# A two-block transformer on one core: the second layer's norm and projection stream by stream, its low-rank chunk third, its convolution later, two ring slots lent, and output products tile by tile

## What is computed

```python
# layer 0 (even): both streams            # layer 1 (odd)
z = h @ w_in                              # h: RMS norm of x, times (1+scale), plus shift
o = window_attention(q, k, v)             # layer 1: mla_q / mla_kv: low-rank parts are RMS-normed, then @ w_uq / @ w_ukv, rope
s = spatial_gating(...)                   # layer 1: gb * conv3(gc * hh)   (gated_short_conv)
x = x + gate * (concat([o, s]) @ w_out)
h = rms_norm(x) * (1 + m4) + m3
x = x + m5 * expert_choice_ffn(h)         # 16 experts, each takes its 32 best tokens of a stream
```

## Time and profile before

| | us |
|---|---|
| median of 3 runs | 2333.02 (2328.42 to 2338.51) |
| the profiled execution | 2334.52 |
| its span | 2332.7 |
| PE busy | 1998.7 (86%) |
| VectorE busy | 1002.4 (43%) |
| ScalarE busy | 749.3 (32%) |
| DMA | 643.78 MB, mean 276 GB/s |

### The profile page before, as it was taken

How to read it: one execution, slowest core, us unless ns; L and a number is a source line. 1 busy time by engine, 2 the same in 40 slices (tenths; PEclk the granted TensorE clock), 3 DMA queues, 4 the chain that set the end, 5 groups by cost and what they waited for, 6 DMA issues and landing times.

```text
span 2332.7 us, 37883 instructions
## 1 busy us (share of the span) xinstructions
PE 1998.7 (86%) x16424; PEld 1492.7 (64%) x16424; DVE 1002.4 (43%) x1908; ACT 749.3 (32%) x1338; POOL 11.3 (0%) x24
## 2 busy tenths in 40 slices
PE   5999899989897889766565656999999999998998
PEld 4777655444443757644444434878888877887887
DVE  3346522222221645411110104665576757556776
ACT  3344310000000625200000003655454546654544
POOL 0000000000000000000000000000000000000000
PEclk9999999999999999888788887999999999999999
DMA  9867379999999523599999995334545443345551
GB/s 398 319 233 308 147 304 427 427 427 427 427 427 427 230 95 124 229 426 427 426 426 427 426 426 230 145 145 148 204 176 194 181 155 134 145 181 190 185 200 66
DMA packets 46147, 643.78 MB, mean 276 GB/s; under 512 B 5232, under 2 KB 5504, under 8 KB 6560
## 3 DMA queue, kind: packets, MB, share of 16 engines
q1 hardware_dynamic: 43776, 628.75, 66.7%
q0 software_dynamic: 2208, 12.62, 1.4%
HBM read 640.30 MB, written 1.05 MB: 275 GB/s over the span
## 4 chain that ended last, share of the span: by engine, by line
PE 64%; DMA 29%; DVE 3%; ACT 2%; issue 1%; SPq 0%; ACTq 0%; DVEq 0%; POOLq 0%
PE bank L918 60%; DMA ring<-in_stream 29%; PE bank L926 3%; DMA arena<-in_b_masks 0%; DVE weights_low L2490 0%; DVE tokens_low L2053 0%; ACT arena L1880 0%; DVE arena L2590 0%; ACT ring L1755 0%; DVE ring L2293 0%; ACT weights_high L1592 0%; ACT arena L1624 0%; DVE x L2104 0%; DVE arena L2220 0%; ACT arena L1613 0%
## 5 line engine op out<-in xcount | busy, mean ns | idle before, releaser
L918 PE MATMUL bank<-ring,arena 128*32 128x128 f32 (+4 forms) x7704 | 621.7, 379 | 213.3 <-DMA ring<-in_stream 208.4
L918 PEld LDWEIGHTS bank<-ring,arena 128*32 128x32 f32 (+1 forms) x7704 | 366.3, 134 | 439.1 <-DMA ring<-in_stream 265.0
L2490 DVE TENSOR_TENSOR weights_low<-ring,weights_high 128x1024 fp32r<-128x1024 f32 (+2 forms) x288 | 343.5, 1195 | 271.9 <-ACT weights_high L1592 268.4
L1592 ACT ACTIVATE weights_high<-ring 128x1024 fp32r<-128x1024 f32 (+2 forms) x288 | 297.7, 1035 | 283.3 <-PE bank L918 282.7
L918 PE MATMUL bank<-weights_high,tokens_high_low 128*128 128x512 f32 (+2 forms) x1152 | 359.2, 386 | 10.7 <-DVE tokens_high_low L2502 8.8
L918 PEld LDWEIGHTS bank<-weights_high,tokens_high_low 128*128 128x128 f32 x1152 | 215.1, 189 | 55.9 <-DVE tokens_high_low L2502 9.2
L1592 ACT ACTIVATE arena<-bank 128x256 f32<-128x256 f32 (+6 forms) x254 | 104.5, 435 | 389.7 <-PE bank L926 301.7
L918 PE MATMUL bank<-weights_low,tokens_high_low 128*128 128x512 f32 (+2 forms) x576 | 218.9, 380 | 0.0
L2210 DVE TENSOR_TENSOR arena<-arena,bank 128x256 f32<-128x256 f32 (+1 forms) x64 | 22.7, 355 | 446.2 <-PE bank L918 446.2
L1716 ACT ACTIVATE arena<-bank 128x256 f32<-128x256 f32 (+1 forms) x64 | 21.2, 331 | 572.9 <-PE bank L918 572.9
L2220 DVE TENSOR_TENSOR arena<-bank,arena 32x512 f32<-32x512 f32 (+1 forms) x128 | 70.8, 553 | 254.0 <-PE bank L918 252.7
(11 more groups left out here) (216 smaller groups left out, 2107.4 us busy)
## 6 DMA issues: line engine op xcount, KB each, us to landing
ring<-in_stream SPq DMA_DIRECT2D x298, 2048.0 KB, 21.8
arena<-in_stream POOLq DMA_DIRECT2D x7, 1024.0 KB, 9.7
x<-in_x_in SPq DMA_DIRECT2D x1, 2048.0 KB, 10.6
arena<-in_od_pack POOLq DMA_DIRECT2D x1, 1024.0 KB, 13.1
x<-in_stream POOLq DMA_DIRECT2D x1, 1024.0 KB, 13.7
arena<-in_gains POOLq DMA_DIRECT2D x2, 512.0 KB, 5.9
out<-arena SPq DMA_DIRECT2D x1, 1024.0 KB, 4.0
arena<-in_b_masks POOLq DMA_DIRECT2D x1, 896.0 KB, 9.6
```

What stands on the lines that cost most here:

```text
L918: ins = pe.matmul(o, lhsT, rhs, start=start, stop=stop)
L1592: ins = act.activation(o, i, ACT.Copy)
L2490: dve.tensor_tensor(dst, whole, high.bitcast(F32), ALU.subtract).then_inc(sig, 1)
```

## The change

The bank table, the order of odz and the ring:

```diff
-ADDS_AT = 42
+ADDS_AT = 40
-ODZ_ORDER = (1, 2, 3, 4, 0)
+ODZ_ORDER = (1, 2, 0, 3, 4)
+ODZ_BANKS = {1: (0, 1), 2: (6, 7), 0: (0, 1, 2, 3), 3: (4, 5), 4: (6, 7)}
+CTX_TURNS = (1, 3)
+LORA_SQUARES, LORA_ROOTS, LORA_SCALES, LORA_ROPE = (2, 3, 4), 5, (6, 7), 1
-RING_SLOTS = (3, 1, 4, 5, 0, 2)
-B2_SLOTS = (0, 2, 3, 1)
+RING_SLOTS = {"moe0": (3, 1, 4, 5, 0, 2), "odd": (2, 3, 1, 0), "moe1": (2, 3, 4, 5, 1, 0)}
+B2_SLOTS = (1, 0, 2, 3)
-OD_WEIGHTS = ((13312, 14336), (7040, 19456), (6528, 22016))
+OD_WEIGHTS = ((7040, 19456), (6528, 22016))     # the third buffer lies in the ring
+od_zb, od_q, od_xn = spare(...)                 # in slots 4 and 5
```

Output products, the last three pieces of c=1 tile by tile (mix0 and mix1), and VectorE's order behind mix0:

```diff
+            def z_tail(name, c):
+                ks = range(KD - LAST_TOGETHER, KD)      # LAST_TOGETHER = 3
+                for t in range(tiles):
+                    for k in ks:
+                        if t == 0:
+                            pe.wait_ge(sem("z_w_lo"), Z_AT[name, c, k] + 1)
+                        ...three products of tile t...
+                used(name, c)
             for t in range(4):
                 mix_add("mix0", 1, t)
-            scaled(X, moe_xn, 4, 8)
+                if t:
+                    scaled(X, moe_xn, 4, 8, [t - 1])
+            scaled(X, moe_xn, 4, 8, [3])
```

From the experts to the projection. PE: the gate rows come in front of the last combine; 16 transposes of the main stream, and those of the context behind piece (1, 3):

```diff
                     elif what == "comb":
+                        if layer == 0 and g == GROUPS - 1:
+                            for n in range(4):
+                                v = 2 + 3 * (n // 2)
+                                mod_row("modrow1", n, mrow[:, 2 * v * P:(2 * v + 2) * P], 0)
                         combine(g)
-            norm("n1_1", xn4, 4, sem("xn"), 12)
+            stream_turns("n1x", 0)
             for what, c, k in odz_schedule():
                 if what == "w":
                     z_product("odz", c, k)
-                    if (c, k) == (0, 2):
-                        convolution()
+                    if (c, k) == CTX_TURNS:
+                        stream_turns("n1c", TT)
```

ScalarE (VectorE has the like: four adds, scale tile 0, two adds, scale tile 1, two adds; `stream_split("n1x")`; scale tiles 2 and 3):

```diff
-            square_sums(X, moe_xn, 4, lambda t: x_done(act, 0, t))
+            b.drained("moe0", (GROUPS - 1, PER_GROUP - 1, "y"))
             for n in range(4):
                 mod_row("modrow1", n)
-            b.drained("modcol1", 1)
-            norm_split("n1_1", A1[1], B1[1], 8, Z_FIRST["odz"])
+            square_sums(X, od_xn, 4, lambda t: x_done(act, 0, t), range(TT))
+            stream_split("n1x", 0, 8)
+            square_sums(X, od_xn, 4, lambda t: x_done(act, 0, t), range(TT, 4))
             for what, c, t in odz_schedule():
                 if what == "w":
                     if not early_split("odz", c, t):
                         z_split("odz", c, t)
+                    if (c, t) == (CTX_TURNS[0], CTX_TURNS[1] + 2):
+                        stream_split("n1c", 1, 16)
+                    if c == 3 and t in LORA_SQUARES:
+                        ...two of the six square sums...
+                    if (c, t) == (3, LORA_ROOTS):
+                        ...two roots...
+            def stream_split(name, s, tok):
+                cols = slice(s * SEQ, (s + 1) * SEQ)          # 256 columns: one stream
+                for half in range(2):
+                    j = 2 * half                              # VectorE: bank j + 1
+                    b.filled(name, j)
+                    for k in (2 * j, 2 * j + 1):
+                        if half:
+                            act.wait_ge(sem("z_tok_lo"), tok + k - 3)
+                        ...scale and shift of k...
+                    for k in range(4 * half, 4 * half + 4):
+                        b.drained(name, k // 2)
+                        copy(z_hi[:, k, cols], z_tokens[:, k % 4, cols], sem("z_tok_hi"))
+                        if s == 0 and k == 1:
+                            ...the two early weight pieces...
```

VectorE scales the low-rank parts at (3, 6) and (3, 7) and ropes the key at (4, 1). Behind the projection PE turns the low-rank parts, then does the convolution, then `uq`:

```diff
+            convolution()
             uq = chunk("odz", 4)[...]
+            pe.wait_ge(sem("conv_done"), TT)                 # in front of attention
+            owed.extend(SPARE_SLOTS)                         # slots 4 and 5 go back
```

More of the change, by code:

```diff
@@ L263, in _tickets @@
             stage("modcol0", [0], LAST_BANK)
[L264 to L267, removed]
+            norm("n1_0")
             for p in range(A_END):
@@ L359, in put @@
         SLOT_OF.append(slot)
-    ring = itertools.cycle(RING_SLOTS)
+    ring = {name: itertools.cycle(slots) for name, slots in RING_SLOTS.items()}
     for c in range(MOD_EARLY):
@@ L378, in _chunks @@
     for key in in_ring + [("mix1", c) for c in range(2)] + [("moe1", k) for k in range(6 * N_EXP)]:
-        put(key, None if key in EXTRA else next(ring))
+        put(key, None if key in EXTRA else next(ring.get(key[0], ring["odd"])))
     first = len(SLOT_OF)
@@ L403, in freed_for @@
 def freed_for(n):
[L405 removed]
+    lent = (SLOT_OF[n] in SPARE_SLOTS) * ((n >= CHUNK_AT["moe0", 0]) + (n >= CHUNK_AT["moe1", 0]))
+    return LOADS_OF[n] - 1 + lent
 def b2_chunk(name, k, layer):
@@ L432, in z_before, with in_tail @@
     return n - Z_BUFS[name] if n - Z_BUFS[name] >= Z_FIRST[name] else None
+LAST_TOGETHER = 3
+def in_tail(name, c, k):
+    return name in ("mix0", "mix1") and c == 1 and k >= KD - LAST_TOGETHER
 def z_width(name, c):
@@ L2018, in _, with scaled @@
             dve.memset(mrow, 0.0).then_inc(sem("mod_clear"), 1)
-            def scaled(x, xn, tiles, n_root):
-                for t in range(tiles):
+            def scaled(x, xn, tiles, n_root, which=None):
+                for t in range(tiles) if which is None else which:
                     dve.wait_ge(sem("root"), n_root - tiles + t + 1)
@@ L2222, in gated_out, with combined @@
                     ins.then_inc(frees(moe, (g, e, "y")), 1)
-                def combined(g):
-                    for n in range(2 * tiles):
+                def combined(g, which=range(2 * tiles)):
+                    for n in which:
                         t, c = n // 2, n % 2
@@ L2237, in experts @@
                         gathered(g)
+                    elif what == "comb" and (layer, g) == (0, GROUPS - 1):
+                        combined(g, range(4))
+                        scaled(X, od_xn, 4, 12, [0])
+                        combined(g, range(4, 6))
+                        scaled(X, od_xn, 4, 12, [1])
+                        combined(g, range(6, 8))
                     elif what == "comb":
@@ L2421, in _ @@
[L2421 to L2426 removed]
+                    if (c, k) == (CTX_TURNS[0], CTX_TURNS[1] + 2):
+                        stream_split("n1c", 1, 16)
@@ new lines, in _ @@
+                    if c == 3 and k in LORA_SCALES:
+                        if k == LORA_SCALES[0]:
+                            dve.wait_ge(sem("lora_root"), 2)
+                            steps.do(dve.reciprocal(rstd2[:, :], ss2[:, :]))
+                        for n in range(3):
+                            lora_scale(3 * LORA_SCALES.index(k) + n)
+                    if (c, k) == (4, LORA_ROPE):
+                        dve.wait_ge(sem("od_in2"), 16)
+                        x = od_za[:, :, KV_LORA:KV_LORA + KR]
+                        tmp = [spare(SPARE_RTMP + 32 * m, TT, 16) for m in range(4)]
+                        rope(x[:, :, 0:16], x[:, :, 16:32], od_cos, od_sin, tmp, sem("od_krope"))
+                        dve.wait_ge(sem("od_krope"), 1)
@@ L2441, in _ @@
                 dve.tensor_copy(kf[:, :, 64:96], over_heads(src, OD_HEADS, KR)).then_inc(sem("od_kr"), 1)
+            for t in range(TT):
+                for part in range(3):
+                    convolve(t, part)
             b.drained("uq", (1, 1))
```

154 lines of the change are left out of this document (99 added, 55 removed).

## The result

| | kernel before | changed kernel | ratio, 95% interval |
|---|---|---|---|
| median of the first measurement (4 runs each) | 2331.07 us | 2315.69 us | 0.9924 (0.9905 to 0.9944) |
| median of the second (9 and 5 runs) | 2333.41 us | 2317.29 us | 0.9927 (0.9915 to 0.9940) |
| span of the profiled execution | 2332.7 us | 2313.8 us | |

What follows compares the result with a forecast made beforehand. Expert stages were taken as bound by the weight stream, so reaching them earlier moves everything after. Gains 3.8 + 2.7 + 5.8 + 0.7 = 13.0 us gave 2320.0 us; the forecast's own range 2315 to 2325, over the cases 2311 to 2330.

Steps and rivals of the forecast that it cites:

- Steps 1: End of mix0: last three pieces run tile by tile, first router norm eviction 3.8 us earlier, bounds 2.5 to 4.5.
- step 5: Low-rank part and convolution, projections' end to first uq eviction: 9.35 us instead of 15.2, gain 5.8, bounds 3.5 to 6.5.
- step 7: Ring of weight slots: two slots lent, cost 0, both expert stages as long as now; 5 to 10 us if chunks were missing.
- Step 6: End of mix1: same tile-by-tile tail with two tiles, gain 0.7 us, bounds 0 to 1.2.
- Step 2: Last expert product to first projection: gate rows before combine, norm split by streams; third piece at 776.8 instead of 781.5, 4.7 gained.
- Step 3: Context stream inside c=1: 1.9 us transposes, 2.7 wait, 1.9 half clock; c=1 ends at 793.4 instead of 791.6.
- Step 4: Projection chunks 2, 0, 3, 4: c=3 1.1 us late from low-rank squares; projections end at 839.0 instead of 841.7, 2.7 gained.
- dearer handoffs: Rival for the projection: ScalarE/VectorE waits come to 11 us instead of 3 + 2.7, 8 lost, 2328; chance 0.15.
- The router's gain: Rival: the router's 3.8 us do not pass on, expert stream bound by loads issued before, 2324; chance 0.06.
- stay at 1.2 GHz: Slower rival: PE stays at 1.2 GHz from piece 2 on, each piece waiting for its weights, 2344; chance 0.08.
- wait elsewhere: Last rival: the squares wait elsewhere and only the low-rank part moves, 2327; chance 0.03.
- hole in the clock: Rival inside c=1: transposes act as a hole in the clock, 12 products by 0.2 us, 2322.5; chance 0.06.

Runs made afterwards that it cites:

- experiment 1: Changed kernel with only the last piece of mix0 and mix1 made for all tiles together again; median 2319.85 us, ratio 0.9950.
- experiment 8: Changed kernel with unused products in PE's two gaps, three before the first projection product and four before the third piece; median 2316.81 us, ratio 0.9930.
- experiment 9: Changed kernel with the low-rank squares, roots, scalings and key's rope behind the whole projection again, convolution left in place; median 2324.48 us, ratio 0.9959.
- experiment 4: Changed kernel with the gate rows behind the combine again and their ScalarE copies behind the squares; median 2317.83 us, ratio 0.9941.
- experiment 5: Changed kernel with the context stream's transposes and split up front, behind the main stream's, instead of inside c=1; median 2313.50 us, ratio 0.9913.
- experiment 7: Changed kernel with the context stream's squares, transposes and halved split spread under the first two projection chunks; median 2310.48 us, ratio 0.9902.
- experiment 2: Kernel before with only the tile-by-tile ends of mix0 and mix1 and scalings between the adds; median 2331.00 us, ratio 0.9989.
- experiments 3: As experiment 2, plus three unused products in PE's wait before the combine; median 2329.71 us, ratio 0.9986.
- 10: As experiment 7, plus three unused products ahead of the first projection product; median 2308.73 us, ratio 0.9891.

## Why the prediction was right, and where it was not

The mechanism held. The time was forecast as 2320.0 and came as 2315.69, inside the forecast's range but 0.7 us from its lower end. Of these 4.3 us, 1.9 are the base (2333.0 then, 2331.07 with the fourth run) and 2.4 the change: -13.0 forecast, -15.4 measured, -16.1 in the second measurement. By the marks, which leave out the start of the run, it is -17.2. Steps 1 (3.8 for 3.9) and 5 (5.8 for 6.15) were right in kind and size, and so was step 7: the expert stages take 469.27 for 469.02 and 459.91 for 459.99 us. Step 6 was forecast as 0.7; up to the norm eviction 0.5 can be seen (93.06 for 93.54), and experiment 1 gives the tile order 0.7. The tile-by-tile ends themselves cost 0.4 us each in the products, where 0.1 and 0.2 had been counted: mix0 22.04 for 21.66, mix1 22.48 for 22.10. The miss by the marks, 4.2 us, is nearly all in steps 2 to 4, where each sum came out too dear (another 0.2 is the old projections' end, read as 841.7 and being 841.89):

- **Step 2, third piece: 1.4.** I had it 27.1 us after the last expert product; it came after 25.7. The first product was 0.55 earlier than worked out. Another 0.55 is in the squares of the context tiles: I took 3.3 for the two with their roots, near the spacing of squares that each wait for their adds; with the data already there they follow each other after 1.37 (765.56, 766.93) and take 2.74. The last 0.3 are in the handoffs.
- **Step 3: 2.0, of which 1.7 the half clock behind the wait.** From the third piece to the end of c=1 it is 14.6 us for 16.6. The wait itself was right, 2.60 for 2.7; the transposes took 1.7 for 1.9. The clock's fall after it, charged at 1.9, did not come; 0.2 remain. It was one of the bounds I had named. But in experiment 8, with pieces 2 and 3 at full clock, the same wait is followed by eight products at half clock: that the term was 0 here was not to be foreseen from the length of the wait.
- **Step 4: 0.5.** Chunks 2, 0, 3 and 4 take 45.06 us for the 45.6 of the sum. The term that was too dear is c=3 being late by the low-rank squares, 1.1: PE does not wait in c=3 (45.06 of 45.10 us busy), and experiment 9, without that work in c=3, ends its projections only 0.4 earlier. By that the squares cost 0.4 where 1.1 had been counted, and the other terms were 0.2 too cheap.

The reasons behind step 2 came out differently from what its text suggests. Of the third piece's 6.1 us, 3.0 belong to the gate rows (experiment 4). Putting the context's work inside c=1 brought the third piece forward, but step 3's costs took all of that back (experiment 5): it could as well have stayed up front. And worked out rather than run: of the 6.9 us from the last expert product to the projections' end, the gate rows' 3.0 and the convolution's 5.3 that moved out of this stretch make 8.3, so that the division by streams with all else there cost about 1.4. No run here has the new order with an undivided norm. Nor does a run move the convolution or chunk 0 back alone: in step 5 the low-rank work is shown by experiment 9, the convolution's place only by the marks.

Of the rivals: dearer handoffs did not occur (2.47 and 2.60 against 3 and 2.7). The router's gain was passed on in full. PE did not stay at 1.2 GHz (granted clock 1.00 from 784.5 on). The squares did not wait elsewhere: all of steps 1 to 5 can be read in the marks. The transposes inside c=1 are no hole in the clock: the products behind those of 774.49 run 0.23 apart. The prediction held that the row of 32 transposes can't tell whether transposes keep the clock; but another such row of the kernel before can. Behind mix0 PE does nothing but 32 transposes from 275.99 to 281.37, and windows inside that row show the clock at full, then at half, then at full again before the row ends (columns as in the earlier trace rows):

```profile
276.00:277.00 1.00, 1.00 (x9) 1.00 (x10) 0.93 (x4) 0.72 (x3) 0.00 (x0) 1.00 0.00 0
277.00:280.00 3.00, 3.00 (x16) 3.00 (x15) 1.48 (x3) 0.00 (x0) 0.00 (x0) 0.50 0.93 268
280.50:281.30 0.80, 0.80 (x8) 0.63 (x6) 0.55 (x2) 0.60 (x2) 0.00 (x0) 1.00 0.95 410
```

The clock rose while PE only transposed. The Trainium skill ("TensorE: Matmul & The Clock Gate", Part 4: PE-mode transpose) says that transposes don't count as activity for the clock gate in the way that products do; this trace does not agree.

Two readings in the recorded text were off without changing a sum. Step 7 calls the DMA at most half busy between the expert stages, but the earlier trace rows have 0.58 and 0.77 there; PE still never waits for a weight chunk in the changed kernel's projection, where its three waits are all for a low half. And among the signs, 769 for the first product leaves out the router's 3.8 while 773 for the third piece already holds it; counted alike they are 765.1 and 773.0, against 762.98 and 770.03, with 1.7 of each difference being the start of the run.

## What to carry over

A step brought forward is worth only what its own remainder leaves: count the work that is pushed behind it, and on which engine it then stands ahead of what. Work that one engine hands to another piece by piece hides under PE only in portions smaller than the lead; where a portion of 5.4 us against a lead of 2.7 cost 2.6, halves cost 0.9, and spread out together with its squares it cost 0.3 (the one wait left in experiment 7). Before crediting a difference between two profiles, find the first mark at which they differ, and whether anything was changed ahead of it.

## What was not expected of the hardware

A wait of PE of about the same length halves the granted clock in one place and not in another: after 2.94 (kernel before), 2.95 (experiment 4) and 2.60 (changed kernel) it stayed full, after 2.95 (experiment 2), 2.61 (experiment 8), 2.47 and 2.71 (changed kernel, before the third piece and the first product) and 2.09 (kernel before, third piece) it fell. In experiment 8 and the changed kernel even the code around the wait is the same; only how PE was filled between the transposes and that wait differs, and there the better filled one fell. What decides it stays open. Nor does the fall always come in the wait: in the kernel before the third piece's first two products, 781.52 and 781.86, still run at the full clock. After 1.34 (experiment 2) and 1.32 (experiment 5) there was none. Filling the wait kept the clock up each time it was tried (experiments 3, 8, 10).
